# Two neighbouring up-projection pairs in one transfer of 4 MB, in the expert part of a decoder step

## The chip, the cores and the metric

The kernel runs on one core of a Trainium2 chip. The metric is the device time of one execution in microseconds (us). Three runs of the kernel before took 1235.82, 1236.94 and 1239.38 us; their median is 1236.94 us. The profile is that of one more execution, which took 1236.71 us. Its span, from the first to the last instruction, is 1234.9 us, so 1.8 us lie around it.

## The reference

One layer of a decoder for 256 prompt tokens and 8 sample tokens, all in float32, with a model width of 1024. A temporal block (sliding-window attention beside a gated recurrent branch) is followed by a layer norm, then by a mixture of experts and a second layer norm. The change lies in the mixture of experts:

```python
logits = (xt @ w_router + b_router)
top_v, top_i = lax.top_k(logits, TOP_K)          # 4 of 32 experts for each token
...
def expert_block(args):                          # up to a block of rows of one expert
    h = xblk @ w_up[e] + b_up[e]                 # w_up[e]: 1024 x 2048
    glu, lin = h[:, :D_FF], h[:, D_FF:]
    act = glu * sigmoid(1.702 * glu) * (lin + 1.0)   # glu and lin clamped before
    return act @ w_down[e] + b_down[e]           # w_down[e]: 1024 x 1024
```

Each expert has 8 MB of up weights and 4 MB of down weights, so the 32 experts bring 384 MB from memory in one execution.

## The kernel before, in words

The first 300 us are the temporal block. Its weights come through a ring of six 1 MB pieces in the buffer `raw`. After it the experts run in passes: 30 passes written out (blocks 0 to 29, expert = block number), a loop of n passes whose experts come from a table (here n is 1), and a last pass that is written out again. A pass takes 64 rows of one expert.

The weights of a pass come as `PER` = 6 transfers of 2 MB, which the code calls pairs: i = 0 to 3 are up weights (`w_up`, 256 rows each), i = 4 and 5 are down weights (`w_down`, 512 rows each). In an up pair each of the 128 partitions holds two neighbouring rows of 8 KB, so one run of 16 KB; in a down pair four rows of 4 KB, again one run of 16 KB. Pairs are numbered on through all passes: q = 6 x block + i. They go round a ring of `NP` = 10 places (lines 284 to 286): places 0 to 6 are the buffer `slots`, places 7 to 9 are made of `raw` when the temporal block is done with it, in the order in which its pieces come free.

All of these transfers are issued by SyncE's queue (SP), one behind the other. Before the transfer of pair q, SP waits until the pair that held the place is used up: the count `used_up`, to which TensorE adds one behind the last matmul of each pair (line 585). Each place has a semaphore of its own for the landing (`ring_loaded`, `place` at line 452), and TensorE waits for it before the first matmul of the pair (`landed` at line 1223).

The order of TensorE's work in a pass is written out in `run` (line 1309): `up` of pair 0, `up` of pair 1 (four `up_rows` each), `combine` (adds the previous pass to the result), `up_end` for pairs 2 and 3 together, the gathering of the next pass's tokens, the transposes of the activations, biases and routes, `down` of pair 4, the transposes of the gathered tokens (`turn_gathered`), `down` of pair 5. `up_end` (line 1245) is ordered so that it can start when pair 2 has landed:

```python
landed(blk, 2)
up_rows(blk, 2, 0, GLU, 0)
up_rows(blk, 2, 1, GLU, 0)
up_rows(blk, 2, 0, LIN, DFF)
landed(blk, 3)
```

Three of its eight `up_rows` (each four matmuls in the trace) thus stand ahead of the wait for pair 3. Pair 2 is used up behind the sixth, pair 3 behind the eighth.

At pair 18 SP also waits for `count_done` and loads the down biases in two small transfers (line 590). In the loop (line 606) SP waits for `used_up` of the pair six places back, since the loop's pairs always use places 0 to 5.

Of the kernel before, what the change touches and what calls it, by code (L numbers as in the profile page):

```python
# [26 lines left out]
P = 128  # L27
D = 1024
# [11 lines left out]
NE, TOPK, DFF = 32, 4, 1024  # L40
# [10 lines left out]
NSTAT = 30  # L51
# [6 lines left out]
RING = 6  # L58
SLOT = 2048
UPP = 4  # L60
PER = 6
NP = 10
# [93 lines left out]
def build(nc, a):  # L156
    chunks, tiles, order, NPC = plan()
    NCH = len(chunks)
# [4 lines left out]
    def flat(name):  # L163
        ap = a[name]
        return ap[0]

    with ExitStack() as whole:
        def sb(name, shape, dt=F32, scope=whole):
            return scope.enter_context(nc.sbuf_tensor(name, shape, dt))

        def sem(name):
            return whole.enter_context(nc.semaphore(name))
# [3 lines left out]
        GLU, LIN, GATH, TURN, ACTT, DOWN, SPOS, SGATE = bank  # L176
# [3 lines left out]
        ident = const[:, C_ID:C_ID + P]  # L180
# [4 lines left out]
        raw = sb("raw", [P, RING, SLOT])  # L185
# [76 lines left out]
        bdown = route[0:2 * NE, 0:512]  # L262
# [9 lines left out]
        gx = sb("gx", [P, 512], scope=late)  # L272
# [9 lines left out]
        slots = sb("slots", [P, NP - RING // 2, 2 * SLOT], scope=late)  # L282
        late.close()
        ring = [slots[:, i, :] for i in range(NP - RING // 2)] \
# [84 lines left out]
        count_done = sem("count_done")  # L369
# [17 lines left out]
        ring_loaded = [sem(f"ring_loaded{i}") for i in range(NP)]  # L387
        used_up = sem("used_up")
# [34 lines left out]
        biases_loaded = sem("biases_loaded")  # L423
# [6 lines left out]
        def slot(c):  # L430
            return raw[:, c % RING, :]
# [8 lines left out]
        Blk = namedtuple("Blk", "first k last")  # L440
        LOOP_PAIR = NSTAT * PER
# [5 lines left out]
        def count(blk, per, extra):  # L447

            value = blk.first * per + extra
            return value if blk.k is None else blk.k * per + value  # L450

        def place(blk, i):

            if blk.last:
                q = LOOP_PAIR + PER + i
                rounds = blk.k + q // NP if q >= LOOP_PAIR + NP else q // NP + 1
            else:
                q = blk.first * PER + i
                rounds = q // NP + 1 if blk.k is None else blk.k + (q // NP + 1)
            return ring[q % NP], ring_loaded[q % NP], rounds * 16  # L460

        def loop_count(e):

            return e.value_load(tablei[0:1, 2 * NLOOP:2 * NLOOP + 1], min_val=1, max_val=NLOOP)
# [22 lines left out]
        def _(sp):  # L487
            wao = flat("w_attn_out").rearrange("(k p) n -> p k n", p=P)
            wro = flat("w_rnn_out").rearrange("(k p) n -> p k n", p=P)
            w_up = a["w_up"].rearrange("l e d n -> (l e d) n")  # L490
            w_down = a["w_down"].rearrange("l e d n -> (l e d) n")

            def used(c):

                if c < NPC:
                    sp.wait_ge(tile_done, max(n for n in range(NT1) if tiles[n][2] == c) + 1)
                elif c < CH_RO:
                    sp.wait_ge(out_done, 2 * (c - CH_AO) + 2)
                elif c < CH_OUT:
                    sp.wait_ge(out_done, 8 + c - CH_RO + 1)  # L500
                elif c < CH_LN:
                    sp.wait_ge(mix_done, c - CH_OUT + 4)
                else:
                    sp.wait_ge(x1_ready, 3)
                    sp.wait_ge(x1_half, 1)


            def expert_pair(blk, i, row0):

                dst, landed, _ = place(blk, i)  # L510
                if i < UPP:
                    src, k = w_up[bass.ds(row0 + i * 2 * P, 2 * P), :], 2
                else:
                    src, k = w_down[bass.ds(row0 + (i - UPP) * 4 * P, 4 * P), :], 4
                sp.dma_start(dst.rearrange("p (k n) -> p k n", k=k),
                             src.rearrange("(p k) n -> p k n", p=P)).then_inc(landed, 16)

            def refill_parts(blk, i, row0):

                dst, _, _ = place(blk, i)  # L520
                return (dst.rearrange("p (k n) -> p k n", k=4),
                        w_down[bass.ds(row0 + (i - UPP) * 4 * P, 4 * P), :].rearrange("(p k) n -> p k n", p=P))
# [56 lines left out]
            for b in range(NSTAT):  # L579
                for i in range(PER):  # L580
                    q = b * PER + i
                    if q < EARLY:
                        continue
                    if q > NP:
                        sp.wait_ge(used_up, q - NP + 1)
                    elif NP > q >= NP - RING // 2:
                        c = NCH - RING + 2 * (q - (NP - RING // 2))
                        used(c)
                        used(c + 1)
                    if q == 3 * PER:  # L590
                        sp.wait_ge(count_done, 1)
                        for h in range(2):
                            sp.dma_start(bdown[h * NE:(h + 1) * NE, :], flat("b_down")[:, h * 512:(h + 1) * 512])\
                                .then_inc(biases_loaded, 16)
                    if q == NP:
                        dst, src = refill_parts(Blk(b, None, False), i, b * D)
                        sp.wait_ge(half_used, 1)
                        sp.dma_start(dst[:, 0:2, :], src[:, 0:2, :]).then_inc(first_refill, 16)
                        sp.wait_ge(used_up, 1)
                        sp.dma_start(dst[:, 2:4, :], src[:, 2:4, :]).then_inc(place(Blk(b, None, False), i)[1], 16)  # L600
                        continue
                    expert_pair(Blk(b, None, False), i, b * D)
            sp.wait_ge(table_ready, 1)
            n = loop_count(sp)
            column = loop_column(sp)
            with sp.Fori(0, n) as k:
                e = sp.value_load(tablei[0:1, bass.ds(column + k, 1)], min_val=0, max_val=NE - 1)
                row0 = e * D
                for i in range(PER):
                    sp.wait_ge(used_up, k * PER + ((NSTAT - 1) * PER + i + 1))  # L610
                    expert_pair(Blk(NSTAT, k, False), i, row0)
            for i in range(PER):
                q = LOOP_PAIR + PER + i
                if q < LOOP_PAIR + NP:
# [3 lines left out]
                if i == PER - 1:  # L618
                    dst, src = refill_parts(Blk(NSTAT, n, True), i, (NE - 1) * D)
# [8 lines left out]
            for q in range(4):  # L628
                c = slice(q * QUARTER, (q + 1) * QUARTER)
# [259 lines left out]
        def _(pe):  # L889
# [52 lines left out]
            for i, (k0, k1) in enumerate(FIRST):  # L942
# [3 lines left out]
                for half in range(2):  # L946
                    for k in range(k0, k1):
                        last = pe.matmul(bank[half][:, 0:T], w[:, k, half * P:(half + 1) * P], xT[:, k, :],
                                         start=k == 0, stop=k == KD - 1)
# [4 lines left out]
            for what, n in order:  # L954
                if what == "tile" and n < 2:
                    continue
                if what == "tile":
                    name, idx, c, half = tiles[n]
# [5 lines left out]
                    if name in ("r", "i"):  # L964
                        pe.wait_ge(conv_ready, idx + 1 if name == "r" else RT)
                        last = pe.matmul(bank[n % 4][:, 0:T], slot(c)[:, idx * P:(idx + 1) * P], xc[:, idx, :],  # L966
                                         start=True, stop=True)
                    else:
                        w = slot(c).rearrange("p (k n) -> p k n", k=KD)
                        for k in range(KD):  # L970
                            last = pe.matmul(bank[n % 4][:, 0:T], w[:, k, half * P:(half + 1) * P], xT[:, k, :],  # L971
                                             start=k == 0, stop=k == KD - 1)
# [16 lines left out]
                elif what == "sample":  # L989
                    if n == 1:  # L990
                        pe.wait_ge(s_qz, 1)
                        pe.wait_ge(o_ready, NPAIR)
                        for b in range(DECB):
                            i, j = b // 4, b % 4
                            last = pe.matmul(bank[6][32 * j:32 * j + 32, i * P:(i + 1) * P], qz[:, b, :], kcT[:, b, :],
                                             start=True, stop=True)
                        last.then_inc(s_sc, 1)
                    elif n == 2:
                        pe.wait_ge(scores_taken, NPAIR)
                        pe.wait_ge(s_pn, 1)  # L1000
                        for i in range(2):
                            last = pe.transpose(bank[4][:, i * P:(i + 1) * P], slog[:, i, :], ident)
                        last.then_inc(s_ptt, 1)
                    elif n == 3:
                        pe.wait_ge(s_pte, 1)
                        pe.wait_ge(s_new, 16)
                        for b in range(DECB):
                            i, j = b // 4, b % 4
                            last = pe.matmul(bank[5][32 * j:32 * j + 32, i * P:(i + 1) * P], pTs[:, b, :], vc[:, b, :],
                                             start=True, stop=True)  # L1010
                        last.then_inc(s_pv, 1)
                    elif n == 4:
                        pe.wait_ge(s_oc, 1)
                        for i in range(2):
                            last = pe.transpose(bank[4][:, i * P:(i + 1) * P], o8[:, i, :], ident)
# [5 lines left out]
            for m in range(16):  # L1021
# [4 lines left out]
                if m < 8:  # L1026
                    c, half = CH_AO + m // 2, m % 2
                    w, src, kk = slot(c).rearrange("p (k n) -> p k n", k=KD), oT, KD
                else:
                    c, half = CH_RO + m - 8, 0  # L1030
                    w, src, kk = slot(c)[:, 0:DR].rearrange("p (k n) -> p k n", k=RT), yr, RT
# [5 lines left out]
                for k in range(kk):  # L1037
                    last = pe.matmul(bank[m % 4][:, 0:T], w[:, k, half * P:(half + 1) * P], src[:, k, :],  # L1038
                                     start=k == 0, stop=k == kk - 1)
# [175 lines left out]
            def turn_gathered(blk):  # L1215

                pe.wait_ge(gx_ready, count(blk, 1, 1))
                for j in range(4):
                    first = (j // 2) * 2 * P + j % 2
                    last = pe.transpose(TURN[:, j * P:(j + 1) * P], gx[:, first:first + 2 * P - 1:2], ident)  # L1220
                last.then_inc(gx_turned, 1)

            def landed(blk, i):
# [139 lines left out]
            n = loop_count(pe)  # L1363
# [603 lines left out]
```

## Time and profile before

| | |
|---|---|
| median of 3 runs | 1236.94 us (1235.82 to 1239.38) |
| profiled execution | 1236.71 us, span 1234.9 us |
| TensorE matmul busy | 1200.4 us (97% of the span), 6419 matmuls |
| DMA moved | 452.00 MB, 366 GB/s over the span |
| up weights, SP queue | 89 transfers of 2048 KB into `slots`, 39 into `raw` |
| down weights, SP queue | 44 and 18 transfers of 2048 KB |
| chain that ended last | PE 75%, DMA 23% of the span |

The busy time of TensorE is a model of pipelined matmuls and says that work was in flight, not that the engine was at its peak. "Time to landing" of a transfer runs from its issue by SP to the last of its completion signals; with several transfers in the queue most of it is the transfers ahead.

### The profile page before, as it was taken

What the parts mean: (1) busy time and instruction counts of PE and PEld (TensorE: products, weight loads), DVE (VectorE), ACT (ScalarE), POOL (GpSimd) and SP (SyncE); (2) the same over time, 40 slices, a digit from 0 to 9 for tenths busy, and PEclk for the clock granted to TensorE, in tenths of its full rate; (3) what the DMA queues carried; (4) which work ended last, traced back from release to release, by engine and by line L of the source; (5) the groups of instructions that cost most, each with busy time, mean ns of one, the idle gap of its engine ahead of it and who ended that gap; (6) DMA issues with size and microseconds to landing.
All of it is one profiled execution on the core that took longest, in us unless ns stands there. A gap on an engine that the chain in (4) does not pass through costs nothing.

```text
span 1234.9 us, 14923 instructions
## 1 busy us (share of the span) xinstructions
PE 1200.4 (97%) x6419; PEld 580.3 (47%) x6419; DVE 375.4 (30%) x844; ACT 197.2 (16%) x425; POOL 9.6 (1%) x15
## 2 busy tenths in 40 slices
PE   9999999999999999999999999999999999999996
PEld 8888888867333343333333333333333333333332
DVE  1467076135322223222222222222222222222223
ACT  1244372001210000101110001110101000000002
POOL 0000000001000000000000000000000000000000
PEclk9999999999999999999999999999999999999999
DMA  9722455973999999999999999999999999999994
GB/s 368 250 98 90 170 205 184 322 276 142 343 417 430 429 430 431 430 429 430 431 430 430 430 429 430 431 431 429 429 431 431 430 429 430 431 431 431 428 430 163
DMA packets 55041, 452.00 MB, mean 366 GB/s; under 512 B 5808, under 2 KB 24432, under 8 KB 26920
## 3 DMA queue, kind: packets, MB, share of 16 engines
q1 hardware_dynamic: 54272, 448.60, 87.8%
q0 software_dynamic: 272, 1.37, 0.3%
q8 instruction: 51, 0.84, 0.3%
q10 hardware_dynamic: 432, 1.08, 0.2%
q14 instruction: 14, 0.11, 0.0%
HBM read 449.70 MB, written 2.45 MB: 366 GB/s over the span
## 4 chain that ended last, share of the span: by engine, by line
PE 75%; DMA 23%; DVE 1%; issue 0%; ACT 0%; ACTq 0%; SPq 0%; DVEq 0%
PE pair L1232 24%; PE pair L1277 15%; PE pair L971 13%; DMA slots<-in_w_up 12%; DMA raw<-in_w_up 10%; PE pair L1038 5%; PE pair L1179 3%; PE pair L1305 3%; PE pair L1262 1%; PE pair L1220 1%; PE pair L1193 1%; PE pair L1057 1%; PE pair L1064 1%; PE pair L1208 1%; PE pair L966 1%; DMA xT<-in_xT 1%
## 5 line engine op out<-in xcount | busy, mean ns | idle before, releaser
L1232 PE MATMUL pair<-slots,xg 128*64 128x512 f32 x1424 | 320.5, 595 | 12.0 <-DMA slots<-in_w_up 11.3
L1232 PEld LDWEIGHTS pair<-slots,xg 128*64 128x64 f32 x1424 | 98.3, 137 | 213.3 <-issue 186.5
L1778 DVE TENSOR_TENSOR xT<-xT,pair 128x528 f32<-128x528 f32 x120 | 76.5, 698 | 394.8 <-PE pair L1305 394.8
L1277 PE MATMUL pair<-slots,at 128*64 128x512 f32 x736 | 167.8, 598 | 0.8 <-ACT at L837 0.8
L971 PE MATMUL pair<-xT,raw 128*128 128x264 f32 x704 | 159.6, 386 | 0.0
L1232 PE MATMUL pair<-raw,xg 128*64 128x512 f32 x624 | 141.1, 595 | 8.4 <-DMA raw<-in_w_up 8.4
L971 PEld LDWEIGHTS pair<-xT,raw 128*128 128x128 f32 x704 | 132.7, 190 | 22.7 <-issue 0.4
L833 ACT ACTIVATE sig<-gsb 128x512 f32<-128x512 f32 x32 | 20.1, 630 | 466.9 <-DVE gsb L1788 466.9
L1277 PEld LDWEIGHTS pair<-slots,at 128*64 128x64 f32 x736 | 48.9, 136 | 92.5 <-issue 80.3
L1232 PEld LDWEIGHTS pair<-raw,xg 128*64 128x64 f32 x624 | 43.1, 137 | 97.2 <-issue 79.9
L1305 PE MATMUL pair<-gt,ysb 64*128 64x264 f32 x496 | 69.4, 409 | 0.0
L1277 PE MATMUL pair<-raw,at 128*64 128x512 f32 x288 | 65.8, 598 | 0.0
L1179 PE MATMUL pair<-xtok,onehot 128*64 128x512 f32 x256 | 60.6, 593 | 1.1 <-DVE onehot L1749 1.1
L1788 DVE TENSOR_SCALAR gsb<-pair 128x512 f32<-128x512 f32 x32 | 22.1, 691 | 128.6 <-PE pair L1232 128.6
L1305 PEld LDWEIGHTS pair<-gt,ysb 64*128 64x128 f32 x496 | 42.7, 186 | 38.5 <-issue 25.0
L837 ACT ACTIVATE at<-pair 128x512 f32<-128x512 f32 x32 | 19.1, 597 | 114.7 <-PE pair L1262 114.7
L824 ACT ACTIVATE xg<-pair 128x512 f32<-128x512 f32 x32 | 19.1, 597 | 113.7 <-PE pair L1220 113.7
L1193 PE MATMUL pair<-bx,bsel 32*64 32x512 f32 x384 | 36.3, 613 | 0.0
L1179 PEld LDWEIGHTS pair<-xtok,onehot 128*64 128x64 f32 x256 | 18.2, 137 | 38.2 <-issue 36.2
L1766 DVE TENSOR_SCALAR gnew<-pair,const 128x264 f32<-128x264 f32 x32 | 15.7, 492 | 66.7 <-PE pair L1208 66.7
L1038 PE MATMUL pair<-yr,raw 128*128 128x264 f32 x160 | 35.8, 386 | 0.0
L1208 PE MATMUL pair<-bx,bsel 32*64 32x264 f32 x256 | 35.4, 394 | 0.0
(306 smaller groups left out, 819.9 us busy)
## 6 DMA issues: line engine op xcount, KB each, us to landing
slots<-in_w_up SPq DMA_DIRECT2D x89, 2048.0 KB, 29.5
slots<-in_w_down SPq DMA_DIRECT2D x44, 2048.0 KB, 33.4
raw<-in_w_up SPq DMA_DIRECT2D x39, 2048.0 KB, 34.8
raw<-in_w_down SPq DMA_DIRECT2D x18, 2048.0 KB, 37.6
raw<-in_w_tiled SPq DMA_DIRECT2D x22, 1024.0 KB, 5.2
raw<-in_w_rnn_out SPq DMA_DIRECT2D x8, 640.0 KB, 11.5
raw<-in_w_attn_out SPq DMA_DIRECT2D x4, 1024.0 KB, 5.0
raw<-in_w_out_tiled SPq DMA_DIRECT2D x4, 1024.0 KB, 4.8
```

The costliest lines, as they stand in the source:

```text
L824: act.activation(xg[:, :, :, :].rearrange("p j h n -> p (j h n)"), TURN[:, :], ACT.Copy)\
L833: act.activation(sig[:, :], gsb[:, :], ACT.Sigmoid, scale=SALPHA).then_inc(sig_ready, 1)
L971: last = pe.matmul(bank[n % 4][:, 0:T], w[:, k, half * P:(half + 1) * P], xT[:, k, :], start=k == 0, stop=k == KD - 1)
L1038: last = pe.matmul(bank[m % 4][:, 0:T], w[:, k, half * P:(half + 1) * P], src[:, k, :], start=k == 0, stop=k == kk - 1)
L1179: ins = pe.matmul(GATH[h * CAP:(h + 1) * CAP, :], onehot[:, t, :], xtok[:, t, h * 512:(h + 1) * 512], start=first, stop=last)
L1193: ins = pe.matmul(to[h * CAP:(h + 1) * CAP, :], bsel[r, :], bx[r, h * 512:(h + 1) * 512], start=first, stop=last)
L1208: last = pe.matmul(to[h * CAP:(h + 1) * CAP, 0:T], bsel[r, :], bx[r, c:c + T], start=True, stop=True)
L1232: last = pe.matmul(to[h * CAP:(h + 1) * CAP, :], xg[:, 2 * (i % 2) + row, i // 2, :], w[:, c:c + 512], start=False, stop=i == UPP - 1 and ...
L1277: last = pe.matmul(DOWN[h * CAP:(h + 1) * CAP, :], at[:, kk, i - UPP, :], w[:, kk * D + h * 512:kk * D + (h + 1) * 512], start=i == UPP an ...
L1305: last = pe.matmul(pair[ADD_PAIR[j]][:, h, 0:T], ysb[h * CAP:(h + 1) * CAP, j * P:(j + 1) * P], gt[h * CAP:(h + 1) * CAP, :], start=not wi ...
L1778: ins = dve.tensor_tensor(y, y, more, ALU.add)
L1788: dve.tensor_scalar(gsb[:, :], GLU[:, :], LIMIT, None, ALU.min).then_inc(glu_taken, 1)
```

## The change

From pair 14 on, two up pairs of one pass that stand in neighbouring places are loaded by one transfer of 4 MB (`expert_quad`), whose runs are 32 KB a partition: partition p takes the four rows 4p to 4p+3 of 512 rows, where before each pair took the rows 2p and 2p+1 of its 256. SP waits until both places are used up, and both pairs wait for the one landing. Where the two places are not neighbours (places 6 and 7, 9 and 0), in the first pass, and in the last, pairs are loaded one by one as before, in the same new order of rows: 16 KB a partition at a step of 32 KB. The columns that the transposes of the gathered tokens take follow the new order of rows. The biases' transfers at pair 18 are issued ahead of the wait for pair 18's place.

```diff
--- before.py
+++ after.py
@@ -449,15 +449,25 @@
             value = blk.first * per + extra
             return value if blk.k is None else blk.k * per + value
 
+        def is_quad(q):
+
+            return q % PER in (0, 2) and NP + 2 < q < LOOP_PAIR + PER and q % NP not in (NP - RING // 2 - 1, NP - 1)
+
+        def signals(q):
+
+            return not (q % PER in (1, 3) and is_quad(q - 1))
+
         def place(blk, i):
 
-            if blk.last:
-                q = LOOP_PAIR + PER + i
-                rounds = blk.k + q // NP if q >= LOOP_PAIR + NP else q // NP + 1
-            else:
-                q = blk.first * PER + i
-                rounds = q // NP + 1 if blk.k is None else blk.k + (q // NP + 1)
-            return ring[q % NP], ring_loaded[q % NP], rounds * 16
+            q = LOOP_PAIR + PER + i if blk.last else blk.first * PER + i
+            by = q if signals(q) else q - 1
+            loads = sum(signals(x) for x in range(by % NP, min(by + 1, LOOP_PAIR), NP))
+            in_loop = [x % NP for x in range(LOOP_PAIR, LOOP_PAIR + PER) if signals(x)]
+            if q >= LOOP_PAIR:
+                loads += 1
+                if not blk.last or by % NP in in_loop:
+                    loads = blk.k + loads
+            return ring[q % NP], ring_loaded[by % NP], loads * 16
 
         def loop_count(e):
 
@@ -505,15 +515,28 @@
                     sp.wait_ge(x1_half, 1)
 
 
+            def up_rows_of(row0, h):
+                return w_up[bass.ds(row0 + h * 4 * P, 4 * P), :].rearrange("(p k) n -> p k n", p=P)
+
             def expert_pair(blk, i, row0):
 
                 dst, landed, _ = place(blk, i)
                 if i < UPP:
-                    src, k = w_up[bass.ds(row0 + i * 2 * P, 2 * P), :], 2
+                    src, k = up_rows_of(row0, i // 2)[:, 2 * (i % 2):2 * (i % 2) + 2, :], 2
                 else:
-                    src, k = w_down[bass.ds(row0 + (i - UPP) * 4 * P, 4 * P), :], 4
-                sp.dma_start(dst.rearrange("p (k n) -> p k n", k=k),
-                             src.rearrange("(p k) n -> p k n", p=P)).then_inc(landed, 16)
+                    src, k = w_down[bass.ds(row0 + (i - UPP) * 4 * P, 4 * P), :].rearrange("(p k) n -> p k n", p=P), 4
+                sp.dma_start(dst.rearrange("p (k n) -> p k n", k=k), src).then_inc(landed, 16)
+
+            def expert_quad(blk, i, row0):
+
+                _, landed, _ = place(blk, i)
+                first = (blk.first * PER + i) % NP
+                if first < NP - RING // 2:
+                    dst = slots[:, first:first + 2, :].rearrange("p a n -> p (a n)")
+                else:
+                    c = (NCH + 2 * (first - NP + RING // 2)) % RING
+                    dst = raw[:, c:c + 4, :].rearrange("p a n -> p (a n)")
+                sp.dma_start(dst.rearrange("p (k n) -> p k n", k=4), up_rows_of(row0, i // 2)).then_inc(landed, 16)
 
             def refill_parts(blk, i, row0):
 
@@ -581,17 +604,23 @@
                     q = b * PER + i
                     if q < EARLY:
                         continue
+                    if q == 3 * PER:
+                        sp.wait_ge(count_done, 1)
+                        for h in range(2):
+                            sp.dma_start(bdown[h * NE:(h + 1) * NE, :], flat("b_down")[:, h * 512:(h + 1) * 512])\
+                                .then_inc(biases_loaded, 16)
+                    if not signals(q):
+                        continue
+                    if is_quad(q):
+                        sp.wait_ge(used_up, q - NP + 2)
+                        expert_quad(Blk(b, None, False), i, b * D)
+                        continue
                     if q > NP:
                         sp.wait_ge(used_up, q - NP + 1)
                     elif NP > q >= NP - RING // 2:
                         c = NCH - RING + 2 * (q - (NP - RING // 2))
                         used(c)
                         used(c + 1)
-                    if q == 3 * PER:
-                        sp.wait_ge(count_done, 1)
-                        for h in range(2):
-                            sp.dma_start(bdown[h * NE:(h + 1) * NE, :], flat("b_down")[:, h * 512:(h + 1) * 512])\
-                                .then_inc(biases_loaded, 16)
                     if q == NP:
                         dst, src = refill_parts(Blk(b, None, False), i, b * D)
                         sp.wait_ge(half_used, 1)
@@ -607,8 +636,12 @@
                 e = sp.value_load(tablei[0:1, bass.ds(column + k, 1)], min_val=0, max_val=NE - 1)
                 row0 = e * D
                 for i in range(PER):
-                    sp.wait_ge(used_up, k * PER + ((NSTAT - 1) * PER + i + 1))
-                    expert_pair(Blk(NSTAT, k, False), i, row0)
+                    if is_quad(LOOP_PAIR + i):
+                        sp.wait_ge(used_up, k * PER + ((NSTAT - 1) * PER + i + 2))
+                        expert_quad(Blk(NSTAT, k, False), i, row0)
+                    elif signals(LOOP_PAIR + i):
+                        sp.wait_ge(used_up, k * PER + ((NSTAT - 1) * PER + i + 1))
+                        expert_pair(Blk(NSTAT, k, False), i, row0)
             for i in range(PER):
                 q = LOOP_PAIR + PER + i
                 if q < LOOP_PAIR + NP:
@@ -1216,8 +1249,7 @@
 
                 pe.wait_ge(gx_ready, count(blk, 1, 1))
                 for j in range(4):
-                    first = (j // 2) * 2 * P + j % 2
-                    last = pe.transpose(TURN[:, j * P:(j + 1) * P], gx[:, first:first + 2 * P - 1:2], ident)
+                    last = pe.transpose(TURN[:, j * P:(j + 1) * P], gx[:, j:4 * P:4], ident)
                 last.then_inc(gx_turned, 1)
 
             def landed(blk, i):
```

## Rows read from the trace of the kernel before

**Rows 1.** The page's slices of the span: what the DMA engines moved, 30.9 us each.

```profile
GB/s 368 250 98 90 170 205 184 322 276 142 343 417 430 429 430 431 430 429 430 431 430 430 430 429 430 431 431 429 429 431 431 430 429 430 431 431 431 428 430 163
```

**Rows 2.** Windows: length, each engine's busy time, granted clock, DMA share, GB/s.

```profile
5.00:10.00 5.00, 4.72 (x22) 3.71 (x21) 0.00 (x0) 0.00 (x0) 0.00 (x0) 1.00 1.04 428
...
510.00:811.00 301.00, 301.00 (x1630) 112.21 (x1628) 76.21 (x154) 33.16 (x56) 0.00 (x0) 1.00 1.01 430
811.00:1176.00 365.00, 345.45 (x1836) 124.43 (x1832) 86.10 (x173) 36.81 (x61) 0.00 (x0) 1.00 1.01 430
```

**Rows 3.** The DMA view of two of these windows: packets and bytes.

```profile
DMA packets 451, 2.14 MB, mean 428 GB/s; under 512 B 48, under 2 KB 48, under 8 KB 325
...
DMA packets 8894, 129.53 MB, mean 430 GB/s; under 512 B 987, under 2 KB 987, under 8 KB 987
```

**Rows 4.** The chain of waits in order of time: start, length, what.

```profile
756.22 6.87 PE pair L1232 x32
...
783.58 6.87 PE pair L1232 x32
...
792.62 7.02 PE pair L1232 x32
...
810.99 41.66 DMA raw<-in_w_up
...
852.69 4.51 PE pair L1232 x20
...
911.38 4.51 PE pair L1232 x20
...
971.12 4.51 PE pair L1232 x20
...
1151.32 25.29 DMA slots<-in_w_up
...
1176.66 4.51 PE pair L1232 x20
...
1188.90 3.58 PE pair L1277 x16
...
1203.65 7.02 PE pair L1232 x32
```

**Rows 5.** The timeline of the SP queue: start, length, line, transfer, count.

```profile
336.57 4.59 SPq L515 DMA_DIRECT2D slots<-in_w_up  x2
344.27 0.33 SPq L515 DMA_DIRECT2D slots<-in_w_down  x1
348.22 0.33 SPq L515 DMA_DIRECT2D raw<-in_w_down  x1
355.69 0.79 SPq L593 DMA_DIRECT2D route<-in_b_down  x2
...
1136.56 15.09 SPq L515 DMA_DIRECT2D slots<-in_w_up  x4
```

**Rows 6.** Line 515 in windows with one issue each: issue, time to landing.

```profile
L515 SPq DMA_DIRECT2D raw<-in_w_up x1: 328/328/328, 310.1 to 310.1; - x1
...
DMA to landing us min/median/max: 7.6/7.6/7.6
...
L515 SPq DMA_DIRECT2D slots<-in_w_up x1: 328/328/328, 340.8 to 340.8; - x1
...
DMA to landing us min/median/max: 10.4/10.4/10.4
...
L515 SPq DMA_DIRECT2D slots<-in_w_up x1: 328/328/328, 368.7 to 368.7; - x1
...
DMA to landing us min/median/max: 12.9/12.9/12.9
```

**Rows 7.** Groups by line: the transposes, count, busy, mean ns, idle before.

```profile
L1262 PE MATMUL pair<-const,lsb 128*128 128x128 f32 x128 | 23.9, 310 | 0.0
L1220 PE MATMUL pair<-const,gx 128*128 128x128 f32 x128 | 23.8, 309 | 0.1
```

## The prediction

> **What bounds the kernel now.** I read the page's slices first. From slice 12 of 40 (371 us) to slice 38 the DMA engines move 428 to 431 GB/s without a dent [rows 1]; two long windows of that time both show 430 GB/s at a DMA share of 1.01 [rows 2]. So the DMA engines are never out of work from there on, although TensorE is busy 97% of the span. The chain of waits shows how both fit. Up to 811 us the chain is TensorE alone, one pass in 783.58 - 756.22 = 27.36 us. From there it leaps from TensorE to a transfer's landing and back: 852.69 to 911.38 is two passes, 29.35 us each, and again to 971.12 [rows 4]. Six pairs of 2 MB at 430 GB/s take 6 x 4.88 = 29.3 us. TensorE began with a full ring, ran 2 us a pass faster than the transfers and from about 811 us on had eaten its lead. The DMA stream therefore sets the time of the last wait, at 1176.6 us (pair 183 of the loop's pass lands: 1151.32 + 25.29), and what TensorE does behind that landing is the tail, 1236.71 - 1176.61 = 60.1 us of the profiled execution [rows 4].
>
> The time is thus (a) when the DMA stream becomes gapless, (b) its bytes by its rate up to pair 183, (c) the tail. Time that TensorE loses or wins in its own stretch before 811 us is worth nothing.
>
> **How much is merged.** Quads start at the even pairs 14 to 184 that have remainder 0 or 2 by 6: 29 + 28 = 57. Those at place 6 are left out, 11 of them. That gives 46 quads, 92 of the 192 pairs, both halves of the loop's pass among them (pairs 180 and 182, places 0 and 2).
>
> **Part 1, a gap at the start (adds).** A quad is issued when its second place is free. SP then holds back not only the first half but everything behind it: the down pairs, the biases and later up pairs. This costs only if the DMA engines run dry. A 2 MB transfer that meets an empty queue lands 7.6 us after its issue (the one at 310.1) [rows 6]; 4.88 of that is data, 2.7 latency. The first quad, pairs 14 and 15, had its halves issued at 336.57 and at about 340.8 [rows 5, 6]; now both go at 340.8, when pass 0's last down pair is used up. On an empty queue it lands at 340.8 + 7.6 + 4.88 = 353.3. Before, its second half landed at 340.8 + 10.4 = 351.2 [rows 6]. The stream is 2.1 us late, and nothing gives that back, since it is gapless from there to the end. The next tight one is pairs 20 and 21, issued at 368.7: empty, it could land at 368.7 + 12.5 = 381.2; its place in the queue was 368.7 + 12.9 = 381.6, now 383.7 [rows 6], so no new gap. Later the queue is deeper (41.7 us to landing at 811 us [rows 4]). In the loop's pass the first quad goes some 4 us after 1136.56 and the second at 1151.3 as its second half did [rows 4, 5]; the landing 25 us after that last issue leaves over 10 us of cover. I take +2.1; the bounds are 0 (if more of the 7.6 us overlaps with the transfer ahead) and +4.3 (the whole delay from 336.57 to 340.8).
>
> The biases (128 KB, 0.3 us of data) now go right behind pair 17 at 348.2, not at 355.69 [rows 5]. They pass only the wait for pairs 18 and 19 on SP; pass 4 needs them, and their bytes are the same. Nothing.
>
> **Part 2, the last quad makes the tail longer (adds).** Where `up_end` waited for pair 3 it had done three of its eight groups of matmuls: behind the landing came 20 matmuls in 4.51 us. Undisturbed it is 32 matmuls in 7.02 us [rows 4]. With pairs 2 and 3 in one quad, pair 2 lands with pair 3, and all 32 stand behind the landing: +7.02 - 4.51 = +2.51 us. In a pass in the middle this is covered by slack. Behind the landing T come 7.02 us, then the rest of the pass (in the tail from 1176.66 + 4.51 = 1181.17 to 1188.90 + 3.58 = 1192.48, 11.3 us [rows 4]), so TensorE is ready at T + 18.3, while the next pass's first quad lands at T + 4 x 4.88 = T + 19.5: a wait of 1.2 us. From there two ups and the combine take about 9 us (783.58 to 792.62 [rows 4]), and the second quad is there 9.8 us later: 0.7 us. The passes keep to the DMA's 29.3 us. Behind pair 183, though, no wait for a landing follows in the chain [rows 4], and TensorE works straight to the end, so there the 2.51 us count in full. Bounds: 0 (if the last pass's own landings take over the chain) and 2.6. I take +2.5.
>
> **Part 3, fewer and longer runs (removes).** The 92 pairs take 92 x 4.88 = 449 us of the stream. What would runs of 32 KB in place of 16 KB be worth? The nearest rows: a window at 5 to 10 us with 451 packets for 2.14 MB, 4.7 KB on average, has 428 GB/s; 510 to 811 us with 16 KB weights (8894 packets, 129.53 MB, completion signals counted) has 430 [rows 2, 3]. From short to threefold longer packets the rate gained 0.5%. If the next doubling gave as much again it would be 0.005 x 449 = 2.1 us, and that is my upper bound; none is the lower one as to run length. Below nothing is possible too: the two-pass stretches of the chain, 58.69 and 59.74 us, differ by 1.05 us in 12 transfers, 0.09 us each [rows 4], so the rate isn't fixed to better than 2%. I take 1.5 us gained, nearer to the upper end, because completion signals go away too.
>
> **Part 4, the transposes.** L1220 now takes every fourth column, as L1262 already does: 309 against 310 ns [rows 7], x128. Nothing.
>
> Sum: 2.1 + 2.5 - 1.5 = +3.1 us. On the profiled execution 1236.71 + 3.1 = 1239.8; on the median of the runs, which lies 0.23 us higher, **1240.0 us**.
>
> **Rivals.**
>
> *No gain from run length, slower.* The engines split the runs, or the rate of 430 GB/s is already the limit: then parts 1 and 2 stay alone, +4.6 us, 1241.5. It decides as soon as part 3 is under 0.9 us. For it: share 1.01 and the flat 428 to 431 of all slices [rows 1, 2]. Against: the small step in rows 2.
>
> *The new order of rows reads slower.* Neighbouring partitions now start 32 KB apart, for split pairs too. If the merged pairs ran as the slower two-pass stretch ran, 0.09 us more each, that is 92 x 0.09 = 8.3 us beside the 4.6: 1249.8. Nothing in the rows has such a step; down pairs and up pairs share one rate today. The Trainium skill (DMA: Bandwidth & Descriptors, Latency and other measured facts) reports lower rates where the row pitch per partition is a large power of two, from 512 KiB upward; no run here shows this, and a pitch of 32 KiB isn't in its list.
>
> *Each transfer has a fixed cost in the queue, faster.* If merging took enough from the stream, TensorE's 27.36 us a pass would bound all passes: the 11 passes from 852.69 to 1176.66 take 29.45 us each [rows 4], and 11 x 2.09 = 23.0 us would go, 1213.9. Against it: 430 GB/s at a share over 1 leaves no room between queued transfers [rows 2]. The Trainium skill (DMA: Bandwidth & Descriptors, Anatomy of one DMA) gives about 2.0 us fixed and bytes at 436 GB/s for a DMA of the gpsimd path; taken as a cost of each queued transfer, 46 fewer would save an estimated 92 us of stream. The trace disagrees: 2 MB would take 6.8 us by it, and the stream has 4.88.
>
> *The two delays are covered.* If the first quad finds the queue still filled, or the last pass hides the longer `up_end`, one of them falls away, +0.6 to +1.0: 1237.7.
>
> **How the numbers follow.** A difference of 0.3%, 3.7 us, is about what can be told from none: faster ends at 1233.2, slower starts at 1240.7. Forecast 0.53 (its own range 1238 to 1242, a fifth of it above 1240.7), no gain 0.22 (most of it slower), slow rows 0.12, covered 0.08, fixed cost 0.05. Slower: 0.11 + 0.16 + 0.12 = 0.39, less 0.02 for rows that are only a little slow, 0.37. Faster: 0.05 + 0.01 of the covered case = 0.06. Within: 0.57. The range is 1236.5 to 1245.5: it leaves out the fixed cost, the larger part of the slow rows and the ends.
>
> **What would show it.** Right: in the trace after, a transfer of 4096 KB issued at 340.8 us that lands near 353, with a dent of about 2 us in the DMA share at 340 to 343; from about 780 us on TensorE waits at the first and third pair of a pass, never at the second and fourth; behind the last wait `up_end` stands as 32 matmuls in 7.02 us, not 20 in 4.51; the window 510 to 811 at 431 to 432 GB/s, with about half as many packets for the up weights. Wrong: a rate in that window under 430 or over 433, a last wait for a landing in the very last pass, or DMA gaps at later quads.

## The result, and the profile after

The changed kernel takes 1242.24 us (median of 9 runs, 1239.11 to 1243.12) beside 1238.09 us of the kernel before in the same runs (1235.30 to 1239.38): a ratio of 1.0026, 95% interval 1.0015 to 1.0037, so 3.2 us slower, 1.9 to 4.6. The differences from before that follow are all made from such a ratio on record and its interval; here the two medians lie 4.1 us apart, which is inside the interval. The forecast was 3.1 us slower and 1240.0 us. Of the 2.2 us by which 1242.24 lies above it, 1.15 are the kernel before itself, whose median is 1238.09 in these runs and was 1236.94 in the three that the forecast started from.

The profiled execution of after took 1242.38 us, its span is 1240.5, and that is 5.6 us more than the span before. Not all of it is the change. The page's slices of after, TensorE's granted clock and what the DMA engines moved (they answer to [rows 1]):

```profile
PEclk9999999999899999999999999999999999999999
...
GB/s 368 248 97 90 170 204 193 318 271 137 323 385 427 434 427 435 428 427 433 430 432 432 430 433 433 430 433 432 427 435 431 430 434 429 432 429 431 431 427 138
```

Slice 11 (310 to 341 us) has a granted clock of 8 tenths, where before all had 9. The windows of after (length, busy time of PE, PEld, DVE, ACT and POOL, granted clock, DMA share, GB/s; the last two answer to [rows 2]):

```profile
310.00:320.00 10.00, 10.00 (x41) 3.85 (x34) 2.30 (x13) 3.88 (x6) 0.17 (x1) 0.66 0.62 224
340.00:350.00 10.00, 10.00 (x53) 3.53 (x53) 0.73 (x5) 1.19 (x2) 0.00 (x0) 1.00 0.77 301
510.00:811.00 301.00, 298.73 (x1617) 111.45 (x1614) 76.27 (x154) 32.66 (x55) 0.00 (x0) 1.00 1.01 431
811.00:1176.00 365.00, 342.94 (x1832) 129.93 (x1830) 83.36 (x168) 37.41 (x62) 0.00 (x0) 1.00 1.00 431
```

From 310 to 320 us the granted clock is 0.66, a mixture of the two levels 1.2 and 2.4 GHz; in the 10 us ahead it is 0.83 already. TensorE runs groups of 2 to 14 short matmuls there, as it does in before, where the clock stays at 1.00 in both windows; why it falls in one execution and not in another isn't shown. Pair 13 lands 2.7 us late for it. The dip comes without quads too: the kernel without any quad (below, `e4`) has 0.66 in the same window, and the kernel before with one wait moved further back (`e8`) has 0.64. The dip is therefore no part of the change, and it is probably what spreads the runs of both kernels over 4 us; what the change does is read behind it, from landing to landing.

The gap at the start: SP's queue in after (start, length, line, transfer, count), and the time to landing of pair 13 and of the first quad (these answer to [rows 5, 6]):

```profile
330.85 2.04 SPq L528 DMA_DIRECT2D slots<-in_w_up  x2
343.89 0.33 SPq L539 DMA_DIRECT2D slots<-in_w_up  x1
...
351.27 0.33 SPq L528 DMA_DIRECT2D raw<-in_w_down  x1
351.64 0.93 SPq L610 DMA_DIRECT2D route<-in_b_down  x2
```

```profile
L528 SPq DMA_DIRECT2D slots<-in_w_up x1: 328/328/328, 332.6 to 332.6; - x1
...
DMA to landing us min/median/max: 11.7/11.7/11.7
```

```profile
L539 SPq DMA_DIRECT2D slots<-in_w_up x1: 327/327/327, 343.9 to 343.9; - x1
...
DMA to landing us min/median/max: 12.3/12.3/12.3
```

Pair 13 lands at 332.6 + 11.7 = 344.2, the quad (pairs 14 and 15) at 343.9 + 12.3 = 356.2: 12.0 us behind it. Before, pair 15 landed at 351.2 and pair 13 at 341.5, 9.7 us apart: two transfers without a gap. That is 2.3 us, but not yet the whole gap: pair 25 lands 62.9 us behind pair 13, before 59.8 us. The dent stands in the window 340 to 350: a DMA share of 0.77. The biases' transfers went behind pair 17 at 351.6, as their new place says.

The stream and the packets (answers to [rows 3]):

```profile
DMA packets 6511, 129.87 MB, mean 431 GB/s; under 512 B 720, under 2 KB 720, under 8 KB 720
```

The same 301 us carry 129.87 MB in 6511 packets, before 129.53 in 8894: the long runs do travel as longer packets.

The chain of waits (answers to [rows 4]):

```profile
732.00 6.87 PE pair L1264 x32
...
759.41 38.88 DMA slots<-in_w_up
798.33 7.11 PE pair L1264 x32
805.46 41.30 DMA slots<-in_w_up
846.89 7.09 PE pair L1264 x32
...
1157.10 22.62 DMA slots<-in_w_up
1179.76 7.09 PE pair L1264 x32
...
1194.58 3.58 PE pair L1309 x16
...
```

Now each leap to a landing is followed by 32 matmuls in 7.1 us: the first or second quad of a pass. The last landing in the chain is the quad of pairs 182 and 183, at 1157.10 + 22.62 = 1179.7, and 32 matmuls stand behind it where 20 stood before; no landing follows in the chain. From there to the end of the span it takes 60.8 us, before 1234.9 - 1176.6 = 58.3. The transposes (answers to [rows 7]) cost 313 and 310 ns:

```profile
L1252 PE MATMUL pair<-const,gx 128*128 128x128 f32 x128 | 24.2, 313 | 0.0
L1294 PE MATMUL pair<-const,lsb 128*128 128x128 f32 x128 | 24.0, 310 | 0.0
```

All profiles by the same marks, each landing read as above, in us (pair 41 is the last one ahead of the first quad of e1 and e3):

| kernel | clock at 310 to 320 us | pair 13 to 15 | pair 13 to 25 | pair 15 to 183 | of it from pair 41 | tail | span |
|---|---|---|---|---|---|---|---|
| before | 1.00 | 9.7 | 59.8 | 825.4 | 696.5 | 58.3 | 1234.9 |
| after | 0.66 | 12.0 | 62.9 | 823.5 | 694.9 | 60.8 | 1240.5 |
| e1 first quad at 42 | 0.76 | 9.7 | 59.8 | 822.8 | 694.8 | 60.8 | 1235.9 |
| e2 pair 182 split | 1.00 | 11.8 | 62.8 | 823.6 | 694.9 | 62.0 | 1238.9 |
| e3 both | 0.69 | 9.7 | 59.8 | 822.9 | 694.9 | 60.3 | 1237.3 |
| e4 no quad | 0.66 | 9.7 | 59.5 | 824.2 | 696.5 | 58.3 | 1236.4 |
| e5 loop in pairs | 0.71 | 11.7 | 62.4 | 823.3 | 694.8 | 58.3 | 1237.8 |
| e6 quads of 16 KB runs | 0.67 | 11.4 | 62.7 | 825.3 | 696.3 | 60.8 | 1242.2 |
| e7 quads where free | 0.66 | 9.7 | 60.4 | 823.3 | 694.5 | 58.3 | 1235.6 |
| e8 late up_end | 0.64 | 9.7 | 59.4 | 824.1 | 695.6 | 60.9 | 1239.5 |
| e9 one quad | 0.66 | 11.9 | 62.8 | 825.3 | 696.6 | 58.3 | 1239.7 |

A single landing can mislead by a microsecond: e8 has no quad, and yet 695.6 us from pair 41 to 183 where before has 696.5. The DMA view between the landings of these two pairs, in before (480.11 to 1176.61 us), after (484.85 to 1179.71) and e8 (482.91 to 1178.54), tells these apart:

```profile
DMA packets 20568, 299.60 MB, mean 430 GB/s; under 512 B 2280, under 2 KB 2280, under 8 KB 2280
...
DMA packets 14976, 299.50 MB, mean 431 GB/s; under 512 B 1655, under 2 KB 1655, under 8 KB 1655
...
DMA packets 20546, 299.25 MB, mean 430 GB/s; under 512 B 2279, under 2 KB 2279, under 8 KB 2279
```

In e8 fewer bytes fell between the two landings; bytes by time are 430.1 GB/s in before, 430.2 in e8 and 431.0 in after. Over all profiles, the five without runs of 32 KB behind pair 41 (before, e4, e6, e8, e9) have 430.1 to 430.3 and the six with them 431.0 to 431.1: a gain of 0.2%, or some 1.4 us of the 1.6.

### The profile page after: what moved, and what is told of

It is laid out like the page before. It is cut to its first block, busy times and chain, and to the rows that moved or that the text cites. A ratio compares the mean times of both kernels' runs of the same rounds, so it can differ in the third digit from the quotient of the medians.

```text
span 1240.5 us, 14871 instructions
## 1 busy us (share of the span) xinstructions
PE 1203.3 (97%) x6419; PEld 588.9 (47%) x6419; DVE 375.0 (30%) x844; ACT 197.3 (16%) x425; POOL 9.6 (1%) x15
## 4 chain that ended last, share of the span: by engine, by line
PE 74%; DMA 25%; DVE 1%; issue 0%; ACT 0%; SPq 0%; DVEq 0%
PE pair L1264 25%; DMA slots<-in_w_up 21%; PE pair L1309 13%; PE pair L1004 13%; PE pair L1071 5%; DMA raw<-in_w_up 3%; PE pair L1212 3%; PE pair L1337 3%; PE pair L1226 1%; PE pair L1252 1%; PE pair L1294 1%; PE pair L1090 1%; PE pair L1097 1%; PE pair L1241 1%; PE pair L999 1%; PE pair L981 1%
## 5 line engine op out<-in xcount | busy, mean ns | idle before, releaser
L1264 PEld LDWEIGHTS pair<-slots,xg 128*64 128x64 f32 x1424 | 102.6, 137 | 213.2 <-issue 203.3
L1212 PE MATMUL pair<-xtok,onehot 128*64 128x512 f32 x256 | 62.4, 608 | 0.0
L1309 PEld LDWEIGHTS pair<-raw,at 128*64 128x64 f32 x288 | 19.1, 136 | 34.7 <-issue 30.8
```

The source lines that it names most:

```text
L1212: ins = pe.matmul(GATH[h * CAP:(h + 1) * CAP, :], onehot[:, t, :], xtok[:, t, h * 512:(h + 1) * 512], start=first, stop=last)
L1264: last = pe.matmul(to[h * CAP:(h + 1) * CAP, :], xg[:, 2 * (i % 2) + row, i // 2, :], w[:, c:c + 512], start=False, stop=i == UPP - 1 and ...
L1309: last = pe.matmul(DOWN[h * CAP:(h + 1) * CAP, :], at[:, kk, i - UPP, :], w[:, kk * D + h * 512:kk * D + (h + 1) * 512], start=i == UPP an ...
```

## The experiments

The theory under test was that of the prediction, with the sizes that the marks of after gave at first: three terms that add up, a gap at the first quad (+2.3), a longer `up_end` behind the last landing (+2.5) and a faster stream (-1.6 to -1.9). All kernels differ from after, unless it says otherwise, in the one line of `is_quad`. The gap was taken as 2.3 us, from pair 15 alone; where an expectation misses by about a microsecond, this is a part of why.

**e1, the first quad later.**

```diff
-            return q % PER in (0, 2) and NP + 2 < q < LOOP_PAIR + PER and ...
+            return q % PER in (0, 2) and 4 * NP < q < LOOP_PAIR + PER and ...
```

> First quad at pair 42, not 14 (39 quads for 46). Theory (three terms: gap at the first quad +2.3 us, longer last up_end +2.5, faster stream -1.9): the gap is gone, since the queue is about 8 us deep at 470 us and the quad's delay 4.3; 7 quads of some 0.04 us each are given up. So 2.5 - 1.6 = +0.9 us against the kernel before, 2 us less than the change. The stream from the first up pairs on to the last wait for a landing is shorter than before by about 1.6 us, the tail behind it stays at 60.8 us. Rival (the early delay costs nothing, the profile's later start is TensorE's clock alone): the same time as the change, +3.

Ratio to before 1.0003 (0.9994 to 1.0012), +0.4 us (-0.7 to 1.5). Pair 15 is 9.7 us behind pair 13 again, pair 25 59.8 us, and the tail is still 60.8. The gap is gone and took about its price with it; the rival's 3 us are excluded.

**e2, the last quad split.**

```diff
+            ... and q != LOOP_PAIR + 2
```

> Pairs 182 and 183 (the third and fourth of the loop's pass) one by one again; 45 quads. Theory of three terms: 20 matmuls stand behind the last wait for a landing again, 4.51 us for 7.02, the tail falls from 60.8 to 58.3 us, and the time is 2.3 - 1.9 = +0.4 us against the kernel before. Rival (the last pass's own landings would take over, so the tail is bound by the stream anyway): the same time as the change.

1.0021 (1.0010 to 1.0032), +2.6 us (1.2 to 4.0): this expectation (+0.4) missed. The tail is 62.0 us, not 58.3. The chain of waits of e2 shows why:

```profile
1144.64 22.54 DMA slots<-in_w_up
...
1167.23 8.78 PE pair L1264 x32
1176.01 2.17 PE pair L1337 x16
1178.18 7.02 PE pair L1264 x32
```

The last landing in the chain is now that of the quad of pairs 180 and 181, at 1167.2. TensorE begins the pass behind it, and has both ups and the combine to do before `up_end`; it gets to `up_end` at 1178.2, when pair 183 has long landed. So each of the pass's two quads makes the tail long by itself: behind the first one the two ups and the combine (9.3 us in e3 below) and 7.0 us stand in the place of 9.7 us of stream and 4.5 of `up_end`, which is 2.1 us. The other 1.7 us are clock: the two ups take 8.78 us here and 7.09 in e3, at a granted clock of 0.69 (in the timed runs that need not be so each time):

```profile
1160.00:1167.00 7.00, 4.96 (x24) 1.61 (x20) 0.00 (x0) 1.20 (x2) 0.00 (x0) 1.00 0.96 412
1167.00:1171.00 4.00, 3.77 (x12) 1.21 (x14) 0.00 (x0) 0.00 (x0) 0.00 (x0) 0.69 1.03 438
```

**e3, both edits.**

> Both edits together: first quad at pair 42, pairs 182 and 183 split, 38 quads. Theory of three terms: only the faster stream is left, 38 quads of 0.04 us: 1.6 us faster than the kernel before, 4.5 us faster than the change. Rival (long runs are worth nothing): equal to the kernel before.

1.0003 (0.9993 to 1.0012), +0.4 us: missed for the same reason. The gap is gone, the stream from pair 41 is 1.6 us shorter, and the tail is 60.3 us behind the first quad of the loop's pass, near the 60.4 that the sum made for e2 gives (58.3 + 2.1). A tail longer by 2.0 and a stream shorter by 1.6 make the +0.4 that was timed. The chain of e3:

```profile
1145.08 22.18 DMA slots<-in_w_up
...
1167.31 7.09 PE pair L1264 x32
1174.40 2.17 PE pair L1337 x16
1176.56 7.02 PE pair L1264 x32
```

**e4, the new order of rows without quads.**

```diff
-            return q % PER in (0, 2) and ...
+            return False
```

> No quad at all: every up pair by itself in the new order of rows (runs of 16 KB at a step of 32 KB), the new columns in the transposes, the biases issued early. Theory of three terms: equal to the kernel before within 0.5 us, 430 GB/s from 510 to 811 us. Rival (the step of 32 KB between partitions reads slower, and long runs gain more than 1.9 us to hide it): slower than the kernel before, by 0.09 us for each of 128 pairs, 11 us, if the step costs what the slower stretches of the stream show.

0.9994 (0.9985 to 1.0004), -0.7 us (-1.9 to 0.5). The step of 32 KB between partitions costs nothing: 696.5 us from pair 41 to 183, to the tenth what it was, and 430 GB/s in the window from 510 us. The early biases and the new columns cost nothing that the time shows either. Its windows show the dip at 310 us with no quad in the program, and no dent in the stream at 340 us:

```profile
310.00:320.00 10.00, 10.00 (x40) 3.80 (x32) 2.39 (x13) 3.88 (x6) 0.26 (x1) 0.66 0.63 224
340.00:350.00 10.00, 10.00 (x53) 3.61 (x54) 0.73 (x5) 1.19 (x2) 0.00 (x0) 1.00 0.99 424
510.00:811.00 301.00, 301.00 (x1630) 112.21 (x1628) 76.29 (x154) 33.09 (x56) 0.00 (x0) 1.00 1.01 430
```

**e5, the whole pass of the loop in pairs.**

```diff
-            ... NP + 2 < q < LOOP_PAIR + PER and ...
+            ... NP + 2 < q < LOOP_PAIR and ...
```

> Both quads of the loop's pass (pairs 180 and 182) one by one again, 44 quads, the first still at pair 14. Theory: with pair 182 alone split, the tail stayed long because pairs 180 and 181 landed together and TensorE, with 9 us of work from there to up_end, reached it too late; with both split, 20 matmuls stand behind the last wait again and the tail from pair 183's landing is 58.3 us, against 60.8 of the change. Gap 2.3, stream -1.8: +0.5 us against the kernel before. Rival (the longer tail comes from something else behind the last landing): the tail stays over 60 us.

1.0018 (1.0009 to 1.0027), +2.2 us (1.1 to 3.3). The mechanism holds, the tail is back at 58.3 us; the time missed: it is about 1.7 us more than the expected +0.5, which lies outside the interval. Some 0.8 of it is the gap, which is 3.1 us and not 2.3 (e9). Its profile is 1.4 us longer than that of e4, which has the same dip: +2.0 for the gap, -0.9 from pair 15 to 183, the rest ahead of pair 13.

**e6, quads of short runs.** The transfer of 4 MB keeps the old order of rows, two runs of 16 KB a partition; the single pairs and the columns of the transposes go back to it too (not shown):

```diff
-                sp.dma_start(dst.rearrange("p (k n) -> p k n", k=4), up_rows_of(row0, i // 2)).then_inc(landed, 16)
+                src = w_up[bass.ds(row0 + i * 2 * P, 4 * P), :].rearrange("(a p k) n -> p a (k n)", a=2, p=P)
+                sp.dma_start(dst.rearrange("p (a n) -> p a n", a=2), src).then_inc(landed, 16)
```

> All 46 quads, each one transfer of 4 MB, but in the old order of rows: two runs of 16 KB a partition. Theory (the gain comes from the length of the runs, as a cost of each packet): pair 41 to pair 183 in the stream takes 696.2 to 696.5 us as before, not the 694.9 of the change; gap and tail as in the change, so +4.5 us against the kernel before. Rival (the gain comes from the smaller number of transfers and their completion signals): 694.9 us, and +3.

1.0053 (1.0040 to 1.0067), +6.6 us (5.0 to 8.3; five runs). The stream from pair 41 to 183 takes 696.3 us: without the long runs the gain is gone, though there are just as few transfers as in after. The window of 301 us:

```profile
DMA packets 8625, 129.49 MB, mean 430 GB/s; under 512 B 720, under 2 KB 720, under 8 KB 720
```

As many completion signals (720 packets under 512 B) as in after, but 7905 data packets for 5791, and 129.49 MB for 129.87. So the gain belongs to the packets, not to the transfers. The time missed: it is 2 us above the expected +4.5, which lies outside the interval. Some 0.8 of it is the larger gap, the rest I can't place.

**e7, quads only where they were thought free.**

```diff
-            ... NP + 2 < q < LOOP_PAIR + PER and ...
+            ... NP + PER < q < LOOP_PAIR and ...
```

> First quad at pair 18, the next one behind the change's first, and none in the loop: 43 quads. Theory: the quad at pair 18 goes to a queue that is still filled, so leaving out one quad takes the whole gap away (pairs 14 and 15 land 9.7 us behind pair 13, not 12.0), the tail is 58.3 us, and only the faster stream is left: 1.8 us faster than the kernel before. Rival (the gap is only put off to the next quad): pair 41 lands 2 us later than before, measured from pair 13, and the time is that of the kernel before.

0.9996 (0.9987 to 1.0005), -0.5 us (-1.6 to 0.6). The time missed: -1.8 us was expected and lies outside the interval, and the time is the rival's, that of the kernel before. Without the single quad at pair 14 most of the gap is gone, though the next quad comes four pairs later. Not all of it: pair 25 lands 60.4 us behind pair 13, where it is 59.4 to 59.8 in the five kernels without a quad up to there and 62.4 to 62.9 in the five with a quad at pair 14. From 360 to 410 us its DMA engines move 0.32 MB less than those of e4 (second line; pair 13 lands at 344.3 in both), which is 0.7 us at 430 GB/s:

```profile
DMA packets 1093, 20.91 MB, mean 418 GB/s; under 512 B 144, under 2 KB 144, under 8 KB 208
...
DMA packets 1544, 21.23 MB, mean 425 GB/s; under 512 B 192, under 2 KB 192, under 8 KB 256
```

The queue was filled again, but thinly: by the timeline of SP the quad of pairs 18 and 19 was issued at 360.6, 3.9 us before the transfer ahead of it landed, and that of pairs 20 and 21 at 372.0, 3.0 us before:

```profile
331.03 13.36 SPq L528 DMA_DIRECT2D slots<-in_w_up  x4
...
360.63 0.35 SPq L539 DMA_DIRECT2D raw<-in_w_up  x1
371.95 0.35 SPq L539 DMA_DIRECT2D slots<-in_w_up  x1
```

The tail has its 20 matmuls again:

```profile
1154.21 23.13 DMA slots<-in_w_up
...
1177.39 4.51 PE pair L1264 x20
```

694.5 us from pair 41 to 183 is the shortest of all, by fewer bytes (299.35 MB) and not by a higher rate (431.0 GB/s); its span is 0.8 us shorter than that of e4. This is the best version with quads that was run, and by the timed runs it can't be told from the kernel before.

**e8, the long tail without quads.** The kernel before, with one wait moved:

```diff
                 landed(blk, 2)
+                landed(blk, 3)
                 up_rows(blk, 2, 0, GLU, 0)
                 up_rows(blk, 2, 1, GLU, 0)
                 up_rows(blk, 2, 0, LIN, DFF)
-                landed(blk, 3)
```

> The kernel before, no quads, with up_end's wait for pair 3 put next to its wait for pair 2 in all passes. Theory: the tail grows by 2.5 us (32 matmuls in 7.0 us behind the last wait for 20 in 4.5) and nothing else changes, since the passes in the middle have the slack: +2.5 us, with the stream's 696.5 us from pair 41 to pair 183. Rival (waiting longer in each pass costs by itself, through later releases or TensorE's clock): more than +3.5, and a longer stream.

1.0020 (1.0008 to 1.0031), +2.5 us (1.0 to 3.8), with a tail of 60.9 us: the price of part 2 by itself, and the passes in the middle cover it. The end of the chain, with the 32 matmuls of `up_end`; pair 183 lands at 1178.54 us, 0.1 us before TensorE gets there, which is a little late in this profile by a lower clock at 1149.5 us (last section):

```profile
1169.60 6.87 PE pair L1232 x32
1176.47 2.17 PE pair L1305 x16
...
1178.68 7.09 PE pair L1232 x32
```

**e9, one quad.**

```diff
-            return q % PER in (0, 2) and ...
+            return q == NP + 4
```

> One quad in the whole program, pairs 14 and 15; all other up pairs one by one in the new order of rows. Theory (the gap is this quad's alone and is never given back): pairs 14 and 15 land 11.4 to 12.0 us behind pair 13, not 9.7; the tail is 58.3 us and pair 41 to pair 183 take 696.5 us as without quads; so +2.0 us against the kernel before. Rival (the stream catches up, since TensorE has a lead of many passes): no difference from the kernel before.

1.0018 (1.0009 to 1.0027), +2.2 us (1.1 to 3.3): one transfer that starts late costs 2 to 3 us at the last wait, some 840 us later. Its profile, beside that of e4 with the same order of rows and the same dip, is 3.3 us longer, and pair 183 lands 3.3 us later. The landings of pair 15 show only 2.2 of it, but pair 25 has 62.8 for 59.5, and from 340 to 360 us the DMA engines move 7.21 MB where those of e4 move 8.59: 3.2 us at 430 GB/s. The whole of the gap is thus about 3.1 us (62.4 to 62.9 beside 59.4 to 59.8). The timeline of SP, with that one quad and pairs again at 358.83, and the last landing in the chain with its 20 matmuls:

```profile
330.94 2.04 SPq L528 DMA_DIRECT2D slots<-in_w_up  x2
343.98 0.33 SPq L539 DMA_DIRECT2D slots<-in_w_up  x1
...
358.83 2.06 SPq L528 DMA_DIRECT2D raw<-in_w_up  x2
```

```profile
1157.05 24.43 DMA slots<-in_w_up
...
1181.53 4.51 PE pair L1264 x20
```

## Why the prediction was right

- *What bounds the kernel.* Shown. A delay of the stream at 344 us is still there at the end (e9), and TensorE's lead of many passes doesn't pay it.
- *Part 1, the gap.* The mechanism is as predicted, its size was too small: 2.1 us by the landing of the first quad, which is indeed 2.3 us later against pair 13, but about 3.1 by pair 25 and by the bytes (e9), inside the stated bounds. It was the only one: from pair 13 to 41 after takes 140.6 us and e9, with no quad behind pair 15, 140.7. So pairs 18 and 20 were covered, as the sum for [rows 6] had it, but because the stream was already late: in e7, without the first gap, they cost 0.7 us.
- *Part 2, the tail.* Predicted 2.51 us; after has 60.8 for 58.3, and e8 alone costs 2.5. What the prediction did not see is that the pass's first quad would cost nearly as much (2.1 us) if the second were split: e2 and e3 found it. For the change itself this made no difference, since the later landing decides.
- *Part 3, the stream.* Predicted 1.5 us, between 0 and 2.1; from pair 41 on 1.6 us are gained by 39 quads, 1.4 of them by the rate. I had given completion signals as a reason for the upper half; e6, which has as few of them, shows that they are worth at most 0.2 us of it and the longer packets the rest. The size came partly from a wrong reason, and otherwise from two windows whose rates differ by 2 GB/s, the smaller of them only 5 us long: that it came out was in good part luck.
- *Part 4 and the biases.* Nothing that can be told, by e4.
- *The rivals.* "No gain from run length" would have had 696.5 us from pair 41; after has 694.9. "The new order of rows reads slower" falls with e4. A fixed cost in the queue would have brought all passes to 27.36 us; from pair 41 on merging took 1.6 us in all. The Trainium skill (DMA: Bandwidth & Descriptors, Anatomy of one DMA) gives about 2.0 us fixed for a DMA of another path; as a cost of each queued transfer no run here shows it. "Covered" falls with e8 and e9.
- *The signs.* The dent, the quad at its issue, the 32 matmuls, and the packets came as named. The quad was issued at 343.9 and not 340.8, by the dip; the chain's first leap to a landing ends at 798 us where 780 was named; and the packets of the up weights fell by 40%, not by half: 2116 fewer (7907 to 5791 data packets), of two thirds of 7907. The forecast had halved all of them, but only four fifths of the up pairs in that window are merged.

The sum of the measured terms is 3.1 + 2.5 - 1.6 = +4.0 us, beside 4.1 between the profiles of after and e4, which have the same dip, and a timed difference of 3.2 (1.9 to 4.6) against before. The forecast's 3.1 us lies so close to the 3.2 partly by luck, since its first term was a microsecond short. With the gap at 3.1 us, and 0.7 of it left in e7, the terms give +3.3 for e2 (without the low clock), +1.3 for e5, +5.6 for e6 and -1.1 for e7, all inside their intervals; e6 still took 1 us more than that, which stays open, as its interval is 3 us wide. The stretch from pair 15 to 41 varies between 127.7 and 129.0 us from profile to profile, with and without quads, so single landings settle no more.

## What to carry to other kernels

Where the transfers set the end, count only what moves the stream: when it becomes gapless, its rate, and the work behind its last landing. A larger transfer is paid at both ends of the stream, at the first one because it waits for more room while the queue is still empty, at the last because more work then stands behind one landing; in the middle, with a deep queue, no cost of it showed. So merge only where the queue is deep, and keep the first and the last passes in small pieces; here even that (e7) brought nothing that the timed runs can tell.

## What the runs showed of the hardware

Doubling runs from 16 to 32 KB in 78 of the 142 pairs from pair 42 to 183 took 1.6 us off 696 (0.2%; 431.0 GB/s for 430.1), and starting neighbouring partitions 32 KB apart in place of 16 took or gave nothing (e4).

In two profiles the granted clock fell after a short idle time of TensorE in the stretch that waits for transfers: in e8, with a wait of 2.0 us before 1149.5 us, it was 0.57 in the 3.5 us behind it.

```profile
1146.00:1149.50 3.50, 1.48 (x12) 0.72 (x9) 2.76 (x5) 0.00 (x0) 0.00 (x0) 1.00 0.97 417
1149.50:1153.00 3.50, 3.50 (x10) 1.33 (x12) 0.00 (x0) 0.00 (x0) 0.00 (x0) 0.57 1.03 440
```

In e2 a wait of 2.3 us was followed by 0.69. In after, a wait of 2.2 us ahead of 1140.6 us was followed by no fall: all of 811 to 1176 us has 1.00. In the two kernels where the clock fell, the matmuls behind the wait took 1.7 us longer each time (4.49 us for 12 beside 2.80 in after, 8.78 for 32 beside 7.09 in e3). What decides between a fall and none isn't shown. In e8 the wait for pair 183 behind it covered the loss but for 0.1 us; in e2, in the last passes, it stands in the tail.
